# A mixture-of-experts router that ranks its logits by pairwise differences, in two halves of the tokens

## What is computed

```python
h = rms_norm(x, norm_ffn_w[layer])
coarse_prob = softmax(h @ wc + bc)                   # 4 groups
g_prob, g_idx = top_k(coarse_prob, 1)                # the best group
fine_logits = (h @ wf + bf).reshape(n, 4, 4)         # 4 experts in each group
fine_sel = fine_logits of group g_idx
e_logit, e_idx = top_k(fine_sel, 2)                  # its two best experts
e_w = softmax(e_logit) * g_prob
x = x + sum over the two: e_w * (silu(gate) * up) @ w_down   # experts of width 256
```

## Time and profile before

| | |
|---|---|
| median of 3 runs | 1202.81 us (1201.9 to 1204.03) |
| span of the profiled execution | 1207.7 us |
| TensorE busy | 1119.9 us, 93% of the span |
| VectorE / ScalarE / GpSimd busy | 687.4 / 596.7 / 416.2 us |
| TensorE's share of the chain that ended last | 86% |

### The profile page before, as it was taken

How to read it: one execution, slowest core, us unless ns; L and a number is a source line. 1 busy time by engine, 2 the same in 40 slices (tenths; PEclk the granted TensorE clock), 3 DMA queues, 4 the chain that set the end, 5 groups by cost and what they waited for, 6 DMA issues and landing times.

```text
span 1207.7 us, 19553 instructions
## 1 busy us (share of the span) xinstructions
PE 1119.9 (93%) x7019; PEld 919.5 (76%) x7019; DVE 687.4 (57%) x977; ACT 596.7 (49%) x873; POOL 416.2 (34%) x348
## 2 busy tenths in 40 slices
PE   6998999999999699998899999999999996999980
PEld 4786887778788588886778888888888885788870
DVE  3434434358743899995617442453432136999975
ACT  4555234251433489996332433233342233899971
POOL 4343311210123144445253335442334331344442
PEclk8998999999999799999899999999999997999995
DMA  9232311112216599995642222322222363999955
GB/s 253 59 86 55 70 38 37 53 36 72 71 26 228 182 342 378 375 366 210 235 131 88 79 79 78 115 88 73 85 70 88 100 193 115 359 374 377 366 205 217
DMA packets 89283, 194.73 MB, mean 161 GB/s; under 512 B 20157, under 2 KB 21241, under 8 KB 88186
## 3 DMA queue, kind: packets, MB, share of 16 engines
q1 hardware_dynamic: 67562, 159.87, 39.6%
q10 hardware_dynamic: 11856, 17.07, 4.1%
q0 software_dynamic: 9792, 16.80, 3.7%
HBM read 189.50 MB, written 23.07 MB: 176 GB/s over the span
## 4 chain that ended last, share of the span: by engine, by line
PE 86%; DVE 6%; ACT 3%; DMA 2%; issue 2%; POOL 1%; POOLq 0%; SPq 0%; DVEq 0%; ACTq 0%
PE ps L663 25%; PE ps L665 24%; PE ps L664 24%; PE ps L2412 2%; PE ps L2204 2%; PE ps L2057 1%; DMA arena<-y 1%; PE ps L2089 1%; PE ps L2340 1%; DMA arena<-hs,slot_rows 1%; DVE arena L1433 1%; DMA x<-in_x_dram 1%; PE ps L2033 1%; PE ps L2020 1%; PE ps L2482 1%
## 5 line engine op out<-in xcount | busy, mean ns | idle before, releaser
L827 POOL TENSOR_TENSOR wl<-raw,wh 128x1024 fp32r<-128x1024 f32 x98 | 238.5, 2441 | 408.4 <-ACT wh L991 408.1
L663 PE MATMUL ps<-wh,hT_hi 128*128 128x512 f32 x864 | 348.2, 403 | 3.9 <-DVE hT_lo L1886 2.4
L665 PE MATMUL ps<-wh,hT_lo 128*128 128x512 f32 x864 | 339.4, 393 | 0.0
L664 PE MATMUL ps<-wl,hT_hi 128*128 128x512 f32 x864 | 338.9, 392 | 0.0
L991 ACT ACTIVATE wh<-raw 128x1024 fp32r<-128x1024 f32 x116 | 122.7, 1068 | 220.2 <-PE ps L665 201.5
L663 PEld LDWEIGHTS ps<-wh,hT_hi 128*128 128x128 f32 x864 | 163.6, 189 | 39.4 <-issue 4.6
L665 PEld LDWEIGHTS ps<-wh,hT_lo 128*128 128x128 f32 x864 | 163.2, 189 | 34.6
L664 PEld LDWEIGHTS ps<-wl,hT_hi 128*128 128x128 f32 x864 | 163.7, 189 | 30.8
L663 PE MATMUL ps<-hT_hi,wh 128*128 128x512 f32 x288 | 117.6, 408 | 8.8 <-ACT arena L1154 6.0
L1861 DVE TENSOR_TENSOR wl<-arena,wh 128x1024 fp32r<-128x1024 f32 x96 | 114.3, 1223 | 5.0 <-ACT wh L1250 2.8
L1861 DVE TENSOR_TENSOR wl<-raw,wh 128x1024 fp32r<-128x1024 f32 x92 | 109.5, 1224 | 11.4 <-ACT wh L991 4.8
(11 more groups left out here) (323 smaller groups left out, 1575.3 us busy)
## 6 DMA issues: line engine op xcount, KB each, us to landing
raw<-in_moe_w_gate_up_dram SPq DMA_DIRECT2D x64, 512.0 KB, 10.7
arena<-in_moe_w_gate_up_dram SPq DMA_DIRECT2D x64, 512.0 KB, 10.3
raw<-in_odd_w_in_dram SPq DMA_DIRECT2D x48, 512.0 KB, 3.7
raw<-in_even_w_in_dram SPq DMA_DIRECT2D x32, 512.0 KB, 4.7
arena<-in_moe_w_down_dram SPq DMA_DIRECT2D x32, 512.0 KB, 11.7
raw<-in_moe_w_down_dram SPq DMA_DIRECT2D x32, 512.0 KB, 14.0
arena<-y ACTq DMA_DIRECT2D x8, 1024.0 KB, 8.4
raw<-in_odd_w_out_dram SPq DMA_DIRECT2D x16, 512.0 KB, 3.5
```

The lines of the kernel that those rows point to most:

```text
L663: nc.tensor.matmul(dst, lh, rh, start=first, stop=False)
L664: nc.tensor.matmul(dst, lh, rl, start=False, stop=False)
L665: return nc.tensor.matmul(dst, ll, rh, start=False, stop=last)
L827: pool.tensor_tensor(columns_of(i, wl[:, i % NSPL, :, :]), raw_columns(i), columns_of(i, wh[:, i % NSPL, :, :]).bitcast(F32), ALU.subtract ...
```

## The change

The router is split into two halves of two row tiles, G = 0 and 1. `ranks(l, G)` on VectorE takes all pairwise differences inside a group of four (logits of the groups, and of the experts of each group), counts for each how many beat it (`beaten_by` holds a tiny negative number where an equal logit of lower index wins, else 0), and marks where 8 x the group's rank + the expert's rank is at most 1. `slots(l, G)` makes the places and one-hots for that half. `places(l, G)` on TensorE counts places for the half. `ranks(l, 0)`, `places(l, 0)` and `slots(l, 0)` stand in `outnorm`, in the output projection; the other half stands in `route` and `moe`. The inputs of the softmax weights and the overflow counts are computed after `rows_known`. On TensorE the transposes of tile 3 move ahead of the logits of tile 2, and `warm(14)` becomes `warm(10)`. On VectorE the norm weight's product of the last row moves ahead of the copy of its transposes. The low parts of pieces m+2 and m+3 move from VectorE to GpSimd, behind the first two gathers. ScalarE gets a Silu of one value behind the router's exponentials. Places now lie in PSUM bank 2, the lists of rows in bank 7.

```diff
 def lo_by_dve(i):
-    return i in DVE_LO or any(m + 2 <= i < m + 6 * NE for m in MOE_PIECE)
+    return i in DVE_LO or any(m + 4 <= i < m + 6 * NE for m in MOE_PIECE)
...
                 gather(0)
                 gather(1)
+                lo(m + 2)
+                lo(m + 3)
...
                 elif step[0] == "moe":
-                    lo(MOE_PIECE[step[1]] + 3)
                     moe(step[1])
...
-                act.wait_ge(s_("r_cexp"), l + 1)
+                act.wait_ge(s_("r_cexp"), 2 * l + 2)
                 A(act.activation(r_a, cd, ACT.Exp), s_("r_exp"))
                 act.wait_ge(s_("r_eexp"), l + 1)
                 A(act.activation(ed, ed, ACT.Exp), s_("r_exp"))
+                A(act.activation(small[:, 414:415], onec, ACT.Silu))
...
                 scaled(l, 2)
+                ranks(l, 0)
                 add(3)
+                D(tt(hrow(NT - 1), X[:, NT - 1, :], wb(2 * l + 1), ALU.mult), s_("norm_w_applied"))
                 name = ("xT", l, 1, NT - 1)
                 tile_is_ready(dve, name)
                 D.read(dve.tensor_copy(hTf[:, 4:8, cols(NT - 1)], v3(tile(name), 4)), name)
-                D(tt(hrow(NT - 1), X[:, NT - 1, :], wb(2 * l + 1), ALU.mult), s_("norm_w_applied"))
+                slots(l, 0)
...
+            def ranks(l, G):
+                Ts = slice(2 * G, 2 * G + 2)
+                dve.wait_ge(s_("norm_r"), 4 * (2 * l + 1) + 2 * G + 2)
+                dve.wait_ge(s_("r_logits"), 2 * l + G + 1)
+                half_lg, half_rank = logit[:, G, :], rank[:, 40 * G:40 * G + 40]
+                raw_lg = sl8[:, Ts, :, :].rearrange("p T j e -> p T (j e)")[:, :, 0:20]
+                D(tt(raw_lg, logits_at[:, G, :, :], rs[:, Ts].unsqueeze(2).broadcast_to([P, 2, 20]), ALU.mult))
+                D(tt(v3(half_lg[:, 0:8], 2), raw_lg[:, :, 0:4], bc_m(bias[:, 0:4], 2), ALU.add))
+                D(tt(v3(half_lg[:, 8:40], 2), raw_lg[:, :, 4:20], bc_m(bias[:, 4:20], 2), ALU.add))
+                of4 = v3(half_lg, 10)
+                D(tt(ahead.rearrange("p (g i j) -> p g i j", i=4, j=4), of4.unsqueeze(2).broadcast_to([P, 10, 4, 4]),
+                     of4.unsqueeze(3).broadcast_to([P, 10, 4, 4]), ALU.subtract))
+                D(tt(v3(ahead, 10), v3(ahead, 10), bc_m(beaten_by, 10), ALU.is_gt))
+                D(dve.tensor_reduce(half_rank, v3(ahead, 40), AX.X, ALU.add))
+                among = v3(ranked, 4)[:, Ts, :]
+                D(stt(v3(ranked[:, 32 * G:32 * G + 32], 8), bc_h8(half_rank[:, 0:8]), 8.0, v3(half_rank[:, 8:40], 8), ALU.mult, ALU.add))
+                D(ts(any80[:, 32 * G:32 * G + 32], ranked[:, 32 * G:32 * G + 32], 1.0, None, ALU.is_le), s_("r_any"))
+                D(tt(oh[:, Ts, :, :], among.unsqueeze(2).broadcast_to([P, 2, 2, NE]),
+                     iota8[:, 0:2].unsqueeze(1).unsqueeze(3).broadcast_to([P, 2, 2, NE]), ALU.is_equal))
+            def slots(l, G):
+                Ts, n = slice(2 * G, 2 * G + 2), slice(4 * G, 4 * G + 4)
+                dve.wait_ge(s_("r_pos"), 2 * l + G + 1)
+                at = v3(place_at[:, 0:64], 4)[:, Ts, :]
+                D(tt(sl8[:, Ts, :, :], oh[:, Ts, :, :], at.unsqueeze(2).broadcast_to([P, 2, 2, NE]), ALU.mult))
+                D(dve.tensor_reduce(slotf[:, n], sl8[:, Ts, :, :].rearrange("p T j e -> p (T j) e"), AX.X, ALU.add))
+                D(tt(hotA[:, n, :].rearrange("p n (j e) -> p n j e", j=2), ..., ALU.mult))
+                D(tt(hotB[:, n, :], ..., ALU.is_equal), s_("r_hot"))
             def route(l):
...
+                ranks(l, 1)
+                slots(l, 1)
+                dve.wait_ge(s_("r_rows"), 2 * l + 1)
+                slot_rows(rows_at, slice(0, NE), s_("rows_known"))
+                for G in range(2):
+                    Ts, c = slice(2 * G, 2 * G + 2), v3(logit[:, G, 0:8], 2)
+                    D(dve.tensor_reduce(mx[:, Ts], c, AX.X, ALU.max))
+                    D(tt(cd[:, Ts, :], c, mx[:, Ts].unsqueeze(2).broadcast_to([P, 2, 4]), ALU.subtract), s_("r_cexp"))
+                    D(tt(sl8[:, Ts, :, :], oh[:, Ts, :, :], v3(logit[:, G, 8:40], 2).unsqueeze(2).broadcast_to([P, 2, 2, NE]), ALU.mult))
+                D(dve.tensor_reduce(top, sl8, AX.X, ALU.add))
+                D(tt(ed, top[:, :, 1], top[:, :, 0], ALU.subtract), s_("r_eexp"))
...
                 D(tt(above, ...)); D(dve.tensor_reduce(ovc, ...)); D(dve.tensor_tensor_scan(ovx, ...))
-                dve.wait_ge(s_("r_rows"), 2 * l + 1)
-                slot_rows(rows_at, slice(0, NE), s_("rows_known"))
...
                 overflow_slots(l)
-                lo_in(m + 2)
-                lo_in(m + 3)
                 overflow_hot()
...
                 finish(3, (3,))
+                places(l, 0)
                 logits(3, (0,))
+                rawT(l, 1, 3)
                 logits(2)
-                rawT(l, 1, 3)
                 logits(3, (1,))
...
+            def places(l, G):
+                c = slice(32 * G, 32 + 48 * G)
+                pe.wait_ge(s_("r_any"), 2 * l + G + 1)
+                mm(place_at[:, c], Lst_b, any80[:, c], start=True, stop=False)
+                for T in range(2 * G + 1 + G):
+                    first = max(2 * G, T + 1)
+                    after = slice(NE * first, c.stop)
+                    n = (c.stop - NE * first) // NE
+                    held = any80[:, NE * T:NE * T + NE].unsqueeze(1).broadcast_to([P, n, NE])
+                    ins = mm(v3(place_at[:, after], n), ones_b, held, start=False, stop=T == 2 * G + G)
+                ins.then_inc(s_("r_pos"), 1)
...
+                places(l, 1)
                 slots_to_rows(rows_at, hotA, empty, 4 * l).then_inc(s_("r_rows"), 1)
-                warm(14)
+                warm(10)
```

More of the change, by code:

```diff
@@ L689, in build @@
         cd = v3(reg(RO + 400, 16), 4)
-        ckey = v3(reg(RO + 416, 16), 4)
-        other = v3(reg(RO + 432, 16), 4)
         r_a = v3(reg(RO + 448, 16), 4)
-        mx, kmax, gp, ed, m1, m2 = (reg(RO + 464 + 4 * n, 4) for n in range(6))
-        fm, fd, fkey = (v3(reg(RO + 488 + 64 * n, 64), 4) for n in range(3))
+        mx, gp, ed = (reg(RO + 464 + 4 * n, 4) for n in range(3))
+        top = v3(reg(RO + 476, 8), 4)
+        ahead, rank, ranked = reg(RO + 2576, 160), reg(RO + 2736, 80), reg(RO + 2816, 64)
         oh = reg(RO + 680, 128).rearrange("p (T j e) -> p T j e", T=4, j=2)
@@ L707, in build @@
         tokv = reg(RO + 1560, 16)
-        first = reg(RO + 1576, NE)
+        beaten_by = reg(RO + 1576, NE)
         hitA = v3(bf(RO + 1592, 8 * (SLOT_TILES - NE)), 8)
@@ L1823, in overflow_hot @@
                 D(tt(hitA, iotaA[:, NE:SLOT_TILES].unsqueeze(1).broadcast_to([P, 8, n7]), slotA.unsqueeze(2).broadcast_to([P, 8, n7]), ALU.is_equal))
-                for j in range(2):
-                    D(tt(hotO[:, :, n7 * j:n7 * (j + 1)], hitA, tokv[:, 8 * j:8 * j + 8].unsqueeze(2).broadcast_to([P, 8, n7]), ALU.mult))
+                D(tt(hotO.rearrange("p n (j e) -> p n j e", j=2), hitA.unsqueeze(2).broadcast_to([P, 8, 2, n7]),
+                     tokv.rearrange("p (j n) -> p n j", j=2).unsqueeze(3).broadcast_to([P, 8, 2, n7]), ALU.mult))
                 for n in (0, 4):
@@ L2057, in logits @@
                             ins = mm(logits_at[:, T // 2, T % 2, :], hTf[:, k, cols(T)], rw[:, k, :], start=k == 0, stop=k == KD - 1)
-                    if T == NT - 1 and halves_of_row[-1] == 1:
+                    if T in (1, NT - 1) and halves_of_row[-1] == 1:
                         ins.then_inc(s_("r_logits"), 1)
@@ L2432, in moe @@
                     tile_is_read(pe, SIDE[SIDE_AT[("xT", l, 1, NT - 1)] - t][0])
-                pe.wait_ge(s_("r_any"), l + 1)
-                mm(ps[:, 7, 0:80], Lst_b, any80, start=True, stop=False)
-                for T in range(NT):
-                    held = any80[:, NE * T:NE * T + NE].unsqueeze(1).broadcast_to([P, NT - T, NE])
-                    ins = mm(v3(ps[:, 7, NE * (T + 1):80], NT - T), ones_b, held, start=False, stop=T == NT - 1)
-                ins.then_inc(s_("r_pos"), 1)
+                places(l, 1)
                 slots_to_rows(rows_at, hotA, empty, 4 * l).then_inc(s_("r_rows"), 1)
-                warm(14)
+                warm(10)
                 def split_ready(n, it):
                     pe.wait_ge(hi_done, it * 12 + (n + 1))
-                    if n < m + 2:
+                    if n < m + 4:
                         pe.wait_ge(lo_pool, lo_count(n))
@@ L2618, in shape_constants @@
     c["c_tok"] = np.concatenate([pair_row.reshape(P, 8), tile_row.reshape(P, 8)], 1)
-    c["c_first"] = np.broadcast_to(np.arange(NE, 0, -1), (P, NE))
+    j = np.arange(EPG)
+    c["c_beat"] = np.broadcast_to(np.where(j[None, :] < j[:, None], -np.finfo(np.float32).tiny, 0.0).reshape(-1), (P, NE))
     e = np.arange(NE)
```

50 lines of the change are left out of this document (13 added, 37 removed).

## The result

The changed kernel took 1208.99 us (median of 5, 1207.49 to 1209.69), beside 1202.81 for the kernel before; the ratio is 1.0044, 95% interval 1.0031 to 1.0057. So it is slower, by 5.3 us by the ratio and 6.2 by the medians. The forecast was 1204.2, no difference that can be measured, with the upper end at 1208.5; the result lies on the slower side, to which I had given 0.41.

A forecast was written before the change was run, and what follows sets the result against it. The first gate-up's start was taken to bound each layer. Twice (-4.0 + 4.1 + 1.8 - 0.4) = +3.0, less 1.6, gave +1.4 us on the 1202.8 us median: 1204.2 us, range 1199.5 to 1208.5.

The forecast's parts named there:

- What bounds it: Expert loop: TensorE is always busy, so whatever moves the first gate-up product moves the layer's end by as much.
- Part 1: Router, logits to rows known: pairwise ranks in two halves make the rows known 4.0 us earlier a layer.
- Part 2: Rows known to first gate-up: VectorE's overflow work, held by GpSimd's two subtractions, loses 4.1 us a layer.
- The 4.9 us that I had named: Loss a layer before the first gate-up if VectorE lost all of both GpSimd subtractions.
- The undisturbed 7.4 us: Time from rows known to first gate-up if GpSimd did not hold VectorE; a gain of 0.25 us.
- Part 3: TensorE's clock: after about 5 us idle, gate-up starts at half clock, losing 1.8 us a layer.
- Part 4: First Silu on ScalarE: loading its table early, by a dummy Silu, gains 0.4 us a layer.
- The 1.6 us on top: Second expert's wait, layer 0 alone: shortened to some 1.45 us, it no longer causes half clock; gain 1.6 us.
- VectorE not held: Rival: GpSimd's subtractions do not hold VectorE, gate-up comes 4.25 us earlier in each layer; 1192 us, chance 0.12.
- The clock holds: Rival: TensorE keeps full clock through the idle time before gate-up; 1200.6 us, chance 0.05.
- The second wait falls to half clock: Rival: the second expert's wait brings half clock in both layers; +5.4 us, 1208.2 us, chance 0.20.
- The half inside pushes the last logits back: Rival: the router half in the output projection only delays the last logits, by 0.4 to 0.6 us; no separate chance.

The follow-up runs named there:

- before_again: Experiment 1: the kernel before, unedited, profiled in a second execution; 1202.79 us, span 1201.0 us.
- experiment 8: `halves_late`: the changed kernel with both weight subtractions on VectorE, and the router's first half moved behind the last logits; 1200.37 us, 0.9972 of the kernel before.
- lo_warm13: The changed kernel with both weight subtractions on VectorE and 13 warming products instead of 10 ahead of the gathered rows; 1195.55 us, 0.9933 of the kernel before.
- experiment 3: The changed kernel with one of GpSimd's two weight subtractions (m+3) moved to VectorE, m+2 left on GpSimd; 1204.69 us, 0.9992 of the kernel before.
- experiment 7: `dummy_first`: the changed kernel with one small product on SBUF operands put directly ahead of VectorE's scan; 1209.7 us in one execution.
- experiment 9: `no_silu`: the changed kernel with both weight subtractions on VectorE and the early dummy Silu left out; 1198.35 us in one execution.
- warm_long: The changed kernel with 20 warming products instead of 4 behind the first transposes on TensorE; 1207.23 us, 1.0017 of the kernel before.
- xt_first: The changed kernel with VectorE's first low half of the gathered rows moved ahead of the overflow slots and one-hots; 1201.34 us, 0.9984 of the kernel before.
- pool_early: The changed kernel with GpSimd's two weight subtractions put ahead of its wait for the rows; 1204.66 us in one execution.
- lo_best: lo_warm13 with the first low half of the gathered rows between the overflow slots and their one-hots on VectorE; 1199.61 us, 0.9964 of the kernel before.

## Why the prediction was right or wrong

**What bounds it: right.** In after, the gate-up product starts when VectorE's first low half is done (L1869, 407.28 to 407.97; gate-up at 408.07), and its start moves the end of the layer: behind the next transposes, layer 0 takes 567.7 to 570.4 us in every run.

**Part 1 (4.0 us gained): right in size.** Rows known are 4.1 us earlier (mean of 18.94 over four layers of before and before_again, 14.82 in after). The sum came out, and the net of the first half too ("nothing lost, little won" at the last logits: 9.6 before, 9.3 after); but experiment 8 shows two larger terms that cancel: the new order ends the logits 1.4 us sooner, and the half inside gives 0.6 to 2.2 us back. That they nearly meet is luck.

**Part 2 (4.1 us lost): right mechanism, term too small.** Two small instructions were to last over 2 us each, with one slipping through between the subtractions; gate-up was to come 11.75 us after the rows. One instruction took 5.36 us, none slipped through, and gate-up came at 12.78 and 12.65: a loss of 5.1 us. The step that failed is where the hold begins. I had it begin when the gathers are shown to end (2.93 us after rows known), with VectorE then on instructions that read PSUM until 3.3; it began with the scan, 2.3 us after rows known, before any PSUM operand could cover it. The sentence that a second subtraction following at once would change the sum "by under 0.1 us" rested on that start. The 4.9 us that I had named for the loss of both subtractions was the better value (5.17 us in the scan). The undisturbed 7.4 us was also summed wrongly: a list of 6.9 us with the low half and 0.1 us behind it, as in the disturbed sum, gives 7.65, and without subtractions on GpSimd the gate-up came at 7.63 in `halves_late` and `lo_warm13`; so without the hold nothing is gained over the kernel before, not 0.25 us. The Trainium skill (SBUF — State Buffer, two separate sides) has the loser of the port pair block for a whole instruction. Experiment 3 agrees, with 3.01 us in the scan beside one subtraction; that an instruction loses two in a row, as in after and in experiment 7 (5.29 us), the page doesn't say.

**Part 3 (1.8 us lost): right in the mean.** Gate-up started at half clock in both layers. From there to the transposes of activations it took 9.73 and 10.88 us, in `lo_warm13`, which starts at full clock, 8.23 and 8.19: 1.5 and 2.7 us. One of the two rows behind it was misread: in before the clock had fallen at 391.8, during the last logits (granted clock 0.80 from 391.5 to 392.0, then 0.50), and not in the idle time from 392.9 on.

**Part 4 (0.4 us gained): right**, 0.5 (wait 1.35 for 1.87, and experiment 9). **The 1.6 us on top: wrong.** In after neither layer fell to half clock at that wait, as forecast, but neither does the second execution of before (experiment 1). I had read the dip from a profiled execution with a longer span (1207.7 us) than any of the 48 timed ones of before in the three series of the experiments (at most 1206.5), booked its absence as a gain, and put the difference on the median. How much of the dip the median holds isn't known; by two falls in six such waits it would be 0.5 us a layer, my estimate.

**The sum** with the measured terms is 2 x (-4.1 + 5.1 + 2.1 - 0.5) = +5.2 us; the ratio gives 5.3 and the medians differ by 6.2. Of the 3.8 us between +1.4 and +5.2, 2.0 are part 2's, 1.6 the dip, the rest parts 1, 3 and 4 (-0.2, +0.6, -0.2). The last 0.1 to 1.0 us isn't located; the stretch behind the router alone scatters by 2.7 us.

**The rivals.** VectorE not held: refuted (5.36 us). The clock holds: refuted (half at gate-up). The second wait falls to half clock: it didn't; the time near its 1208.2 came by another way. Where that wait was 1.28 to 1.35 us, in 18 layers of nine executions, no fall followed. The half inside pushes the last logits back: it does, as experiment 8 shows, at a price inside part 1's net. The median lies 0.5 us above the range; by the ratio, 1208.1 us on the median of before, it is just inside. That it comes so near is luck: the upper end was drawn from a rival that didn't happen. It went past the forecast because the terms of part 2 and the dip both erred to the fast side.

## What to carry to other kernels

Before an operation on two SBUF operands is left to GpSimd, look at what VectorE does at that moment, and price it at the whole duration of all such operations in a row, from the end of what stands ahead of them on GpSimd or sooner: here two of them, off every path by themselves, undid a gain of 4 us a layer, and on VectorE, behind the urgent step, they cost nothing that shows (TensorE's next wait stayed at 1.34 us). And look at more than one execution before you book a stall as a gain: a term read from a profile that is slower than the median may not be in the median.

## What the runs showed of the hardware

- VectorE was held before GpSimd's subtraction is shown to start. At 0.19 us the scan of after would have ended at 397.82, and the subtraction is shown from 398.23; in layer 1 it is 1009.74 and 1010.03; in `dummy_first` the small product would have ended at 398.04, and the subtraction is shown from 398.46. The Trainium skill (Perfetto Trace Analysis, GPSIMD Engine Instruction) advises to treat a GpSimd span in a profile as unreliable; here VectorE was held 0.3 to 0.4 us or more ahead of its shown start, and that decided which instruction was caught.
- Who comes between two waiting subtractions differs. Behind the second gather VectorE got nothing in (pairs of 4.65 to 4.70 us in after, `warm_long`, `xt_first` and `dummy_first`); in `pool_early` it got one instruction in (2.13 and 2.25 us), as in the earlier trace rows (0.69 us became 2.81). In all cases of the first kind VectorE's instruction started while the gather was still shown to run; whether that is the cause wasn't tried.
- In `pool_early` an instruction with one tensor operand (L1782, 128x32) was held for 2.25 us as well (0.18 alone), not only those with two.
- The length of a wait alone didn't settle the clock behind it: after 1.86 or 1.87 us it fell to half in one layer of before and one of `no_silu`, and not in the other layer of each, nor in before_again; after 2.83 us in `lo_best` it fell in layer 1 and not in layer 0.
